# The sample heads of a hybrid decoder step: column groups for the query products, row groups for the state updates

## The reference

```
s   = einsum('bhtd,bhsd->bhts', q, k) * w_intra
num = w_inter * einsum('bhtd,bhde->bhte', q, C) + einsum('bhts,bhse->bhte', s, v)
den = w_inter * einsum('bhtd,bhd->bht', q, n) + sum(s, -1)
h   = num / max(|den|, exp(-m_t))
C_new = decay * C + einsum('bhs,bhsd,bhse->bhde', w_end, k, v)
n_new = decay * n + einsum('bhs,bhsd->bhd', w_end, k)
```

## Time and profile before

| | us |
|---|---|
| median of 3 runs | 2017.78 (2017.48 to 2020.28) |
| the profiled execution | 2021.31 |
| its span, first to last instruction | 2019.6 |
| PE busy | 1958.2 (97%) |
| DVE busy | 705.3 (35%) |
| ACT busy | 449.3 (22%) |
| POOL busy | 119.3 (6%) |

### The profile page before, as it was taken

The page is one execution under the profiler, slowest core; times in us unless marked ns, Lnnn a source line. Parts: engine busy times, 40 slices in busy tenths (PEclk is TensorE's granted clock), DMA queues, the critical chain, the costliest instruction groups (busy, mean ns, idle before and its releaser), DMA issues.

```text
span 2019.6 us, 28454 instructions
## 1 busy us (share of the span) xinstructions
PE 1958.2 (97%) x11637; PEld 1857.1 (92%) x11637; DVE 705.3 (35%) x1268; ACT 449.3 (22%) x704; POOL 119.3 (6%) x246
## 2 busy tenths in 40 slices
PE   7999999999999999799899999999999999999997
PEld 5899999999999999566598999999999999999997
DVE  5311110012332333244535473442443343244236
ACT  5321211133333333311212122111111111111113
POOL 0010046010000000131100000000000000000000
PEclk9999999999999999899999999999999999999999
DMA  9653344342333332776453401111111111111112
GB/s 337 215 172 127 122 139 150 106 138 79 101 101 102 110 111 91 173 228 201 157 191 108 155 22 53 43 42 42 52 42 42 42 42 52 42 42 42 48 35 89
DMA packets 227632, 211.12 MB, mean 105 GB/s; under 512 B 13595, under 2 KB 203919, under 8 KB 227567
## 3 DMA queue, kind: packets, MB, share of 16 engines
q1 hardware_dynamic: 218381, 176.29, 28.8%
q10 hardware_dynamic: 7786, 29.57, 3.6%
q0 software_dynamic: 1408, 4.46, 0.7%
HBM read 156.00 MB, written 54.41 MB: 104 GB/s over the span
## 4 chain that ended last, share of the span: by engine, by line
PE 93%; DVE 3%; DMA 2%; ACT 2%; issue 1%; SPq 0%; ACTq 0%; DVEq 0%
PE dense L1839 80%; PE misc L2184 2%; PE misc L2171 2%; PE misc L2088 1%; PE misc L2092 1%; PE dense L2248 1%; PE misc L1928 1%; PE misc L2061 1%; PE misc L2090 1%; PE dense L1896 1%; DMA cs<-in_state_mlstm_c_dram 1%; PE dense L1988 0%; PE misc L2069 0%; PE misc L1945 0%; DMA xtok<-in_x_sample_dram 0%
## 5 line engine op out<-in xcount | busy, mean ns | idle before, releaser
L1839 PE MATMUL dense<-act_hi,w_hi 128*128 128x384 f32 (+1 forms) x2616 | 617.1, 342 | 12.8 <-DVE act_lo L1264 7.2
L1839 PE MATMUL dense<-act_lo,w_hi 128*128 128x384 f32 (+1 forms) x2616 | 585.0, 330 | 0.0
L1839 PE MATMUL dense<-act_hi,w_lo 128*128 128x384 f32 (+1 forms) x2616 | 584.7, 330 | 0.0
L1839 PEld LDWEIGHTS dense<-act_hi,w_hi 128*128 128x128 f32 x2616 | 450.8, 189 | 38.3 <-issue 24.4
L1839 PEld LDWEIGHTS dense<-act_hi,w_lo 128*128 128x128 f32 x2616 | 449.3, 189 | 8.0 <-issue 8.0
L1839 PEld LDWEIGHTS dense<-act_lo,w_hi 128*128 128x128 f32 x2616 | 448.4, 189 | 6.7 <-issue 6.7
L1249 DVE TENSOR_TENSOR w_lo<-raw,w_hi 128x1024 fp32r<-128x1024 f32 x131 | 160.9, 1228 | 504.5 <-ACT w_hi L836 504.4
L836 ACT ACTIVATE w_hi<-raw 128x1024 fp32r<-128x1024 f32 x132 | 139.8, 1059 | 287.5 <-PE dense L1839 286.9
L1839 PE MATMUL dense<-a_hi,w_lo 128*128 128x384 f32 (+1 forms) x480 | 106.3, 329 | 0.0
L1839 PE MATMUL dense<-a_lo,w_hi 128*128 128x384 f32 (+1 forms) x480 | 105.7, 328 | 0.0
L1775 DVE SCALAR_TENSOR_TENSOR hmT<-dense,mod,hmT 128x768 f32<-128x768 f32 x80 | 81.3, 1017 | 69.3 <-PE dense L1839 68.8
(11 more groups left out here) (308 smaller groups left out, 1591.9 us busy)
## 6 DMA issues: line engine op xcount, KB each, us to landing
z_scratch<-stage ACTq DMA_DIRECT2D x52, 544.0 KB, 2.7
raw<-in_w_in_dram SPq DMA_DIRECT2D x53, 512.0 KB, 3.6
raw<-in_w_gate_up_dram SPq DMA_DIRECT2D x44, 512.0 KB, 3.6
ada_w<-in_w_ada_dram SPq DMA_DIRECT2D x20, 1024.0 KB, 7.0
stage<-z_scratch SPq DMA_DIRECT2D x24, 544.0 KB, 3.8
raw<-in_w_down_dram SPq DMA_DIRECT2D x22, 512.0 KB, 3.5
oin<-z_scratch SPq DMA_DIRECT2D x16, 544.0 KB, 4.5
qkv<-z_scratch SPq DMA_DIRECT2D x8, 1024.0 KB, 6.0
```

What stands on the lines that cost most here:

```text
L1839: ins = pe.matmul(tile(k, c), w[:, off:off + P], x[:, xr, t0:t1], start=(first and p == 0), stop=(last and p == 2))
```

## The change

Tokens of the sample group, where they are rows, are spread over 128 partitions in four groups of 32 (JW), 16 of them used (JV): group j holds the sequences 2j and 2j + 1.

- Query-state products: 32-column weights `qm[:, r, a, j, :]` (r tells the two sequences of a group apart) and the output on partitions 32j to 32j + 31 of the bank, 256 columns, for C; then the same sixteen products with one column of nH for n. n no longer lies in cs.
- Scores, wexpS, argS and pTS have 128 padded columns, the scores in four products; hsS, hnS, hfS and smS have 128 partitions.
- State updates: kb has four blocks of 64 rows; the lower 32 rows of block j hold sequence j, the upper 32 sequence j + 4. The two 32-row groups write to the two banks, and both halves a of a state stand in one bank of 512 columns. So the rounds of a head are 13 in place of 21, DVE adds 512 columns at a time, and four branch passes follow each four updates.
- The new n is a product of ks with wmask in round 3, added to the decayed n by DVE (nW).
- States, and with them q, k and n, are laid with key 2p + a on partition p, so that a partition's two state rows are one run of 2 KB.
- DVE's first copy of a head no longer waits for the states; PE's scores wait for POOL's preparation (`head_prep`).
- hmT is copied from the turned head in two instructions. scol is read by 10 DMAs and set to 1.0 first.

The core of the diff, in order: constants, helpers, SP, POOL, ACT, DVE, PE; context is left out.

```
+NJ, JW, JV = 4, 32, SMP // 4
...
-RPH = 21
+RPH = 13
...
+def padded(ap, j=JV):
+    return ap.rearrange("p (j m) -> p j m", m=JW)[:, :, 0:j]
+def state_round(h, b):
+    return R_SMP + RPH * h + 4 + 2 * (b % NJ) + b // NJ
...
-    sp.dma_start(qkvs[:, s, 2 * g:2 * g + 2, :],
-                 z[2 * h + zr:2 * h + zr + 2, :, SEQ:T].rearrange("j p t -> p j t")
-                 ).then_inc(head_rows_in[s], 16)
+    src = z[2 * h + zr:2 * h + zr + 2, :, SEQ:T]
+    src = (src.rearrange("j p t -> p j t") if zr == Z_V else
+           src.rearrange("j p t -> (j p) t").rearrange("(p a) t -> p a t", a=2))
+    sp.dma_start(qkvs[:, s, 2 * g:2 * g + 2, :], src).then_inc(head_rows_in[s], 16)
-    sp.dma_start(cs[s][:, b, :, 0:HD], state_c[0, b, h].rearrange("(a p) e -> p a e", p=P)
+    sp.dma_start(cs[s][:, b, :, :], state_c[0, b, h].rearrange("(p a) e -> p a e", a=2)
-for a in range(2):
-    wait_full(sp, round_free, R_SMP + RPH * h + 4 + 2 * b + a)
-sp.dma_start(c_s[0, b, h].rearrange("(a p) e -> p a e", p=P), cs[s][:, b, :, 0:HD]
+wait_full(sp, round_free, state_round(h, b))
+sp.dma_start(c_s[0, b, h].rearrange("(p a) e -> p a e", a=2), cs[s][:, b, :, :]
...
-head_store(h % 2, h, b)
+head_store(h % 2, h, j // 2 + NJ * (j % 2))
-head_store(h % 2, h, b)
+head_store(h % 2, h, j // 2 + NJ * (j % 2))
-wait_full(sp, round_full, R_SMP + RPH * h + 20)
+wait_full(sp, round_full, R_SMP + RPH * h + 12)
...
-pool.tensor_tensor(argS[:, s, :], row(negg_s, h), maskS[:, :], ALU.add).then_inc(head_prep, 1)
+pool.tensor_tensor(padded(argS[:, s, :]), row(negg_s, h).rearrange("p (j m) -> p j m", j=NJ),
+                   maskS[:, :].rearrange("p (j m) -> p j m", j=NJ), ALU.add).then_inc(head_prep, 1)
-pool.tensor_scalar(wmask[:, s, :], blk[:, :], curC[:, s, 3:4], None, ALU.mult
+pool.tensor_scalar(wmask[:, s, :], blk[:, :], curC[0:SMP, s, 3:4], None, ALU.mult
-for b in range(NB):
-    pool.tensor_copy(qm[:, b, :, NT * b:NT * b + NT], qkvs[:, s, 0:2, NT * b:NT * b + NT]
-                     ).then_inc(head_prep, 1)
+for r in range(2):
+    for a in range(2):
+        pool.tensor_copy(qm[:, r, a, :, NT * r:NT * r + NT],
+                         qkvs[:, s, a, :].rearrange("p (j r t) -> p j r t", j=NJ, t=NT)[:, :, r, :]
+                         ).then_inc(head_prep, 1)
-pool.wait_ge(head_prep, h * 11 + 11)
+pool.wait_ge(head_prep, h * 7 + 7)
-for b in range(NB):
-    pool.tensor_scalar(kb[:, b, :], ks[:, :], wmask[:, s, b:b + 1], None, ALU.mult
+for j in range(NJ):
+    pool.tensor_scalar(kb[:, j, :], ks[:, :], wmask[:, s, NB + j:NB + j + 1], None, ALU.mult
...
-act.wait_ge(head_prep, h * 11 + 11)
-act.activation(wexpS[:, s, :], argS[:, s, :], ACT.Exp, bias=curC[:, s, 0:1]).then_inc(weights_exp, 1)
+act.wait_ge(head_prep, h * 7 + 7)
+act.activation(wexpS[:, s, :], argS[:, s, :], ACT.Exp, bias=curC[0:SMP, s, 0:1]).then_inc(weights_exp, 1)
-act.activation(hsS[:, :], bank(rb + 2, E1, SMP), ACT.Copy, scale=curC[:, s, 1:2]
+act.activation(hsS[:, :], bank(rb + 2, E1), ACT.Copy, scale=curC[:, s, 1:2]
-wait_full(act, round_full, rb + 20, i, 2 * RPH)
-act.activation(hmT[:, ds(h * 2, 2), SEQ:T], bank(rb + 20, 128).rearrange("p (j t) -> p j t", t=SMP),
-               ACT.Copy).then_inc(round_free[(rb + 20) % 2], 1)
+wait_full(act, round_full, rb + 12, i, 2 * RPH)
+ht = hmT[:, ds(h * 2, 2), SEQ:T].rearrange("p j (g m) -> p j g m", m=JV)
+hp = bank(rb + 12, 2 * P).rearrange("p (j g m) -> p j g m", j=2, m=JW)[:, :, :, 0:JV]
+for a in range(2):
+    ins = act.activation(ht[:, a, :, :], hp[:, a, :, :], ACT.Copy)
+ins.then_inc(round_free[(rb + 12) % 2], 1)
...
-dve.wait_ge(states_in[s], i * (NB * 16) + NB * 16)
-dve.tensor_copy(cs[s][:, :, :, HD], by_head(nT)).then_inc(n_ready, 1)
+dve.tensor_copy(nH[:, s, :, :], by_head(nT)).then_inc(n_ready, 1)
-dve.scalar_tensor_tensor(out=pTS[:, :], in0=bank(rb, SMP, SMP), scalar=HD ** -0.5,
+dve.scalar_tensor_tensor(out=pTS[:, :], in0=bank(rb, P, SMP), scalar=HD ** -0.5,
+dve.wait_ge(n_ready, h + 1)
+dve.wait_ge(head_prep, h * 7 + 7)
+link(dve.tensor_tensor(nW[:, :, :], nH[:, s, :, :],
+                       curD[:, s, :].unsqueeze(2).to_broadcast([P, NB, 2]), ALU.mult))
-dve.tensor_tensor(hnS[:, :], bank(rb + 3, E1, SMP), hsS[:, :], ALU.add
-                  ).then_inc(round_free[(rb + 3) % 2], 1)
-wait_full(dve, round_free, rb + 3, i, per)
+link(dve.tensor_tensor(hnS[:, :], bank(rb + 3, E1), hsS[:, :], ALU.add))
+dve.tensor_tensor(by_head(nO), bank(rb + 3)[:, E1:E1 + 2 * NB].rearrange("p (a b) -> p b a", a=2),
+                  nW[:, :, :], ALU.add).then_inc(round_free[(rb + 3) % 2], 1)
...
-        for b in range(NB):
-            for a in range(2):
-                r = 4 + 2 * b + a
-                full(r)
-                dve.scalar_tensor_tensor(out=cs[s][:, b, a, :], in0=cs[s][:, b, a, :],
-                                         scalar=curD[:, s, b:b + 1], in1=bank(rb + r, E1),
-                                         op0=ALU.mult, op1=ALU.add).then_inc(round_free[(rb + r) % 2], 1)
-            if b == 4:
+        dve.wait_ge(states_in[s], i * (NB * 16) + NB * 16)
+        for q in range(NB):
+            b, r = q // 2 + NJ * (q % 2), 4 + q
+            full(r)
+            dve.scalar_tensor_tensor(out=cs[s][:, b, :, :], in0=cs[s][:, b, :, :],
+                                     scalar=curD[:, s, b:b + 1],
+                                     in1=bank(rb + r).rearrange("p (a e) -> p a e", a=2),
+                                     op0=ALU.mult, op1=ALU.add).then_inc(round_free[(rb + r) % 2], 1)
+            if q == 3:
-            if b == 1:
+            if q == 1:
-        for r in (18, 19):
-            wait_full(dve, round_free, rb + r, i, per)
-        dve.tensor_copy(by_head(nO), cs[s][:, :, :, HD]).then_inc(nO_ready, 1)
+        wait_full(dve, round_free, rb + 3, i, per)
+        dve.sem_inc(nO_ready, 1)
-    leave(H // 2, 14)
+    leave(H // 2, 18)
-dve.tensor_copy(nout[:, :], bank(R_NOUT, HD, HC)).then_inc(round_free[R_NOUT % 2], 1)
+dve.tensor_copy(nout[:, :].rearrange("r (p a) -> r a p", a=2),
+                bank(R_NOUT, HD, HC).rearrange("r (a p) -> r a p", a=2)).then_inc(round_free[R_NOUT % 2], 1)
...
-qs, kks, vvs = (qkvs[:, s, 2 * g:2 * g + 2, :] for g in range(3))
+kks, vvs = (qkvs[:, s, 2 * g:2 * g + 2, :] for g in (1, 2))
+pe.wait_ge(head_prep, h * 7 + 7)
-for a in range(2):
-    ins = pe.matmul(bank(rb, SMP, SMP), kks[:, a, :], qs[:, a, :], start=(a == 0), stop=(a == 1))
+for r in range(2):
+    for a in range(2):
+        ins = pe.matmul(bank(rb, P, SMP), kks[:, a, :],
+                        qm[:, r, a, :, :].rearrange("p j m -> p (j m)"),
+                        start=(r == 0 and a == 0), stop=(r == 1 and a == 1))
...
-pe.wait_ge(head_prep, h * 11 + 11)
-for b in range(NB):
-    for a in range(2):
-        ins = pe.matmul(bank(rb + 2, E1, SMP), qm[:, b, a, :], cs[s][:, b, a, :],
-                        start=(b == 0 and a == 0), stop=(b == NB - 1 and a == 1))
+for lo, hi in ((0, HD), (HD, E1)):
+    for r in range(2):
+        for a in range(2):
+            for j in range(NJ):
+                b = 2 * j + r
+                x = cs[s][:, b, a, :] if lo == 0 else nH[:, s, b, a:a + 1]
+                ins = pe.matmul(misc[JW * j:JW * j + JW, (rb + 2) % 2, lo:hi], qm[:, r, a, j, :], x,
+                                start=(r == 0 and a == 0), stop=(r == 1 and a == 1))
+pe.wait_ge(head_keys, h + 1)
-give(pe.matmul(bank(rb + 3, E1, SMP), pTS[:, :], vs[:, :], start=True, stop=True), rb + 3)
+pe.matmul(bank(rb + 3, E1), pTS[:, :], vs[:, :], start=True, stop=True)
+for a in range(2):
+    c0 = E1 + NB * a
+    ins = pe.matmul(misc[:, (rb + 3) % 2, c0:c0 + NB], ks[:, P * a:P * a + P], wmask[:, s, 0:NB],
+                    start=True, stop=True)
+give(ins, rb + 3)
-for b in range(NB):
+for j in range(NJ):
+    pe.wait_ge(head_kb, h * NJ + (j + 1))
+    take_s(rb + 4 + 2 * j)
+    take_s(rb + 5 + 2 * j)
-        r = rb + 4 + 2 * b + a
-        if a == 0:
-            pe.wait_ge(head_kb, h * NB + (b + 1))
-        take_s(r)
-        give(pe.matmul(bank(r, E1), kb[:, b, P * a:P * a + P], vs[:, :], start=True, stop=True), r)
-        branch(8 + 2 * b + a, 9 + 2 * b + a)
+        for g in range(2):
+            r, rows = rb + 4 + 2 * j + g, slice(SMP // 2 * g, SMP // 2 * g + SMP // 2)
+            ins = pe.matmul(misc[:, r % 2, HD * a:HD * a + HD], kb[rows, j, P * a:P * a + P],
+                            vs[rows, 0:HD], start=True, stop=True)
+            if a == 1:
+                give(ins, r)
+    branch(8 + 4 * j, 12 + 4 * j)
-take_s(rb + 20)
+take_s(rb + 12)
-    ins = pe.transpose(misc[:, (rb + 20) % 2, SMP * a:SMP * a + SMP], hfS[:, P * a:P * a + P],
-                       ident[0:SMP, 0:SMP])
-give(ins, rb + 20)
+    ins = pe.transpose(misc[:, (rb + 12) % 2, P * a:P * a + P], hfS[:, P * a:P * a + P], ident[:, :])
+give(ins, rb + 12)
```

More of the change, by code:

```diff
@@ L212, in trunk @@
         smp = ExitStack()
-        kb = sb(smp, "kb", [SMP, NB, HD])
-        hsS = sb(smp, "hsS", [SMP, E1])
```

(48 more changed lines are left out.)

28 lines of the change are left out of this document (17 added, 11 removed).

## The result

The changed kernel takes 1986.9 us (median of 4 runs, 1985.0 to 1988.4) against 2019.0 us for the kernel before (2017.5 to 2023.1): ratio 0.9837, 95% interval 0.9819 to 0.9855. It is faster by 32 us, 16 us short of the forecast of 1971. The profiled execution took 1987.7 us (span 1985.5), to be held against 1974.6 in the prediction's sum; so 13.1 us have to be found.

A forecast was written before the change was run, and what follows sets the result against it. TensorE, busy 97%, was taken to bound the kernel. Savings of 35.1 us (heads 1 to 3) and 11.9 (head 0), less 0.3, made 46.7: 2021.3 to 1974.6 profiled, forecast 1971 us as median, range 1963 to 1988.

The forecast's parts named there:

- the prediction's sum: Savings over all heads, 46.7 us off the profiled execution's 2021.3 us, giving 1974.6 us.
- F: From the previous head's transposes to the first query-state product, 3.74 us before; forecast to lose 0.4 us.
- A: The query-state products of a head: from 7.07 us to 2.7, 4.4 us saved.
- C: The product of pTS with vs, with the products for n added: 0.58 us becomes 1.05.
- a place of updates: Four state updates issued together in two overlapping row groups: 1.06 us, or 1.92 without overlap.
- four passes: The four branch passes that follow each four state updates: 2.19 us.
- E: A head's state updates with the branch passes between them: from 21.23 us to 13.0, 8.2 us saved.
- rival (3): Evictions of the PSUM banks bound the state updates: 2 us a head lost, 1978 us; chance 0.04.
- rival (1): Row groups do not overlap in the updates: 16.5 us there in all four heads, 1985 us; chance 0.18.
- (4): Slower: each step between groups costs 0.2 us and groups do not overlap, 9 us lost a head, 2053; chance 0.03.
- A to D: Query-state products, three branch passes, pTS product, two branch passes; in head 0 forecast to run from 849.4 to 858.0.
- Rival (2): DMA or SyncE sets the heads' pace, branch weights late: 2 to 3 us a head, 1979 us; chance 0.14.

The follow-up runs named there:

- e9: e2's kernel with all query-state records sent to one column group and all updates reading one row group's rows: 2010.0 us.
- e12: The changed kernel with the states laid out as before the change, two pieces of 1 KB to a partition: 1990.2 us.
- e4: The changed kernel with kb and hsS moved off the prompt states' memory, so ScalarE and GpSimd need not wait for those stores: 1987.1 us.
- e2: The changed kernel with the second share's store issued ahead of the rows and states of the head after next: 1978.8 us.
- e1: The changed kernel with only the load of the branch weights issued one turn of SyncE's loop earlier: 1988.0 us.
- e11: The changed kernel with the four stores of the prompt's n left out: 1978.5 us (two runs).
- e10: e2's kernel with head 0 freed (waits removed, transfers moved), and gate rows and branch weights loaded ahead of the 2 MB of states: 1972.5 us.

## Why the prediction was right, and where its size was off

**TensorE's terms.** Each came out as worked out or a little better, as head 1 shows. F took 3.96 (forecast 4.14), A 2.12 (2.7; the one-column records, 0.4, lie behind the wide ones), C 0.97 (1.05), a place of updates 1.06 (1.06), four passes 2.18 (2.2), E 12.89 (13.0), the head 22.85 (23.8). An eviction of 512 columns took 0.744 (0.75) and kb 0.93 (0.91): no place waited for them, so rival (3) falls. Rivals (1) and (4) fall with e9: without overlap a head takes 32.1, with it 22.9. The estimate of 0.8 us from the Trainium skill (TensorEngine Tiling (Array Packing), Instruction Overhead) lies between the two measured ends: 32 one-column records take 0.4 in four groups and 1.07 in one (e9).

**Head 0.** The first update was forecast for 858.0 and came at 858.34, by the landing that was named. What failed is the path of TensorE up to it. The prediction had A at the low clock from 849.4, so that A to D filled the time to 858.0 and E followed at the full clock, and held that an earlier start of the products brings nothing. They started at 844.97, A to D were done by 851.0, TensorE stood for 7.34 us, and the updates and passes took 15.6 us at 0.81 for 13.0: 2.6 us. A shorter stand costs as much: in e12, with the products at 849.52 behind a wait of 4.65 us, it is 2.39 us and E takes 16.0; in e4, with none, 12.9.

**Heads 2 and 3.** Here lies the miss: the sum gave each head TensorE's own time, and put the waits on SyncE's queue at nothing. Rival (2) had the mechanism, place and transfer (the branch weights behind share and gate rows), but with a chance of 0.14 and at 2 to 3 us a head. Head 2 lost 8.6 us to head 1: 6.8 - 0.5 = 6.3 of waiting, and 2.2 from the first query-state record to the first place (8.24 for 6.00), at the low clock. Head 3 lost 5.6: 4.2 and 1.4. Two things made it larger than priced. The delay from a head's end to the issue of the weights was taken over from the kernel before, 15.7 us; in the shorter heads, with the DMA engines fuller and the stores landing later, it was 22.8, and the landing took 7 us for 4.7. And a late transfer costs more than its lateness: the split, the table load, wexpS and pTS follow it one by one, and TensorE comes back at the low clock.

**The account.** Against the sum of the prediction: head 0 +2.5, head 1 -0.9, heads 2 and 3 +7.6 and +4.7, together 13.9 for the 13.1 us missing; 0.8 came back outside the heads. e2 shows the last two terms by giving them back in its profiled execution, and e4 the clock's part of the first (E in 12.9 us). The result lies 1.1 us inside the stated range, whose high end was made of rival (1), 14 us that did not come, and of rival (2) at its smaller price; that it holds is in part luck.

**Not settled:** why e1's gate rows came 5.6 us later with only 512 KB more ahead of them (the share's store was issued 2.7 us later, and took 9.1 us to land for 6.5), why e2's queue frees head 3 in one execution and not in another, and how many records TensorE holds back for a group.

## What to carry to other kernels

When the bounding engine's work in a loop shrinks by a third, write down the turn of the queue that feeds it, each wait and landing in order, and compare its length with the new loop: slack measured in the long loop is gone in the short one. Put transfers in the order in which they are wanted, and a store that someone waits for ahead of bulk loads. Time saved ahead of a pacing queue was worth nothing here until the queue moved too (e4, 0 us alone; in e11, where SyncE's issue moves with the head, and in e10, where the queue is mended, the gain stays).
